# Hymba trunk, eight cores: mixing products on half the array's columns, weight casts two events behind their load, the last tile's output by quarters

## The reference: what is computed

```python
proj = h @ w_in[l]                       # 2048 -> 5632 columns: q | k | v | gate_a | u | v_s | gate_b
# group A: attention over the last 128 positions, 16 query heads, 4 key heads, RMS norm per head,
#          ALiBi penalty, a learned sink per head; the result times silu(gate_a)
# group B: u = gelu(z_u), v = gelu(z_v), 16 heads of 64 channels, chunks of 128 positions
mixed = einsum('hts,bnshc->bnthc', tril(w_s), v) + b_s      # one 128x128 matrix per head
sgu = u * mixed * silu(gate_b)
x = x + concat([attn, sgu]) @ w_out[l]
```

## Time and profile before

| | us |
|---|---|
| unprofiled runs | 7987.17, 8267.01, 8987.27 |
| median of these | 8267.01 |
| the profiled execution, its own time | 7963.68 |
| its span on the slowest core (core 5), first to last instruction | 7962.0 |
| spans of the eight cores | 7927.1 to 7962.0 |
| PE busy | 7752.7 (97%) |
| ACT busy | 3153.9 (40%) |
| DVE busy | 2864.1 (36%) |
| POOL busy | 645.4 (8%) |

### The profile page before, as it was taken

One profiled execution on the slowest core, in us unless ns is written; L12 is line 12 of the kernel. 1 busy time (PEld: TensorE's weight loads), 2 busy tenths in 40 slices (PEclk: granted clock), 3 DMA queues, 4 the chain that ended last, 5 costly groups with the idle time before them and its releaser, 6 DMA issues.

```text
span 7962.0 us, 140270 instructions; the slowest of 8 cores (7927.1 to 7962.0 us)
## 1 busy us (share of the span) xinstructions
PE 7752.7 (97%) x51494; PEld 4698.3 (59%) x51494; DVE 2864.1 (36%) x4126; ACT 3153.9 (40%) x5272; POOL 645.4 (8%) x622
## 2 busy tenths in 40 slices
PE   5899999999999999999999999999999999999999
PEld 3456555556666655666566665556666666665555
DVE  2523333433333334323333333344323433233333
ACT  1334444433333344434443344444433443233332
POOL 0000000000000000000000000000000000000000
PEclk8999999999999999999999999999999999999999
DMA  9988877786776777887876678777886665555554
GB/s 271 305 279 266 263 252 248 253 253 239 244 249 233 249 250 251 267 282 257 256 256 228 239 255 266 245 251 247 273 257 222 222 229 198 205 188 201 185 181 159
DMA packets 394284, 1925.05 MB, mean 242 GB/s; under 512 B 33680, under 2 KB 37904, under 8 KB 202768
## 3 DMA queue, kind: packets, MB, share of 16 engines
q1 hardware_dynamic: 346640, 1815.92, 69.1%
q10 hardware_dynamic: 46976, 100.17, 3.5%
HBM read 1650.68 MB, written 265.29 MB: 241 GB/s over the span
## 4 chain that ended last, share of the span: by engine, by line
PE 89%; DMA 5%; ACT 2%; SPq 1%; DVE 1%; issue 1%; ACTq 0%; DVEq 0%; POOL 0%
PE pp L283 87%; PE pp L286 2%; SPq L289 1%; DMA m_wslot<-scr 1%; DMA m_cst<-w_in 1%; DMA m_cst<-w_out 1%; ACT m_hb L274 1%; DVE m_qs L274 1%; DVE m_hb L274 0%; DMA m_xs<-x 0%; ACT m_sqf L274 0%; ACT m_cb L274 0%; ACTq L289 0%; DMA m_xr<-w_in 0%; DMA m_wslot<-w_out 0%
## 5 line engine op out<-in xcount | busy, mean ns | idle before, releaser
L283 PE MATMUL pp<-m_hT,m_wslot 128*128 128x512 bf16 (+1 forms) x13824 | 2849.1, 365 | 55.8 <-ACT m_ex L274 17.5
L283 PE MATMUL pp<-m_wslot,m_hT 128*128 128x256 bf16 x21344 | 2373.3, 273 | 37.8 <-DVE m_wslot L274 24.2
L283 PEld LDWEIGHTS pp<-m_wslot,m_hT 128*128 128x128 bf16 x21344 | 2089.6, 98 | 292.0 <-issue 40.3
L283 PEld LDWEIGHTS pp<-m_hT,m_wslot 128*128 128x128 bf16 x13824 | 1351.1, 98 | 1422.5 <-issue 115.2
L274 DVE TENSOR_TENSOR m_tf<-pp,m_bias 64x512 f32<-64x512 f32 (+1 forms) x576 | 373.0, 648 | 2303.7 <-PE pp L283 2239.1
L274 DVE TENSOR_TENSOR m_xr<-m_xr,pp 128x512 f32<-128x512 f32 x1064 | 705.2, 680 | 1009.9 <-PE pp L283 1008.2
L283 PE MATMUL pp<-m_wslot,m_zu 128*128 128x512 bf16 x4256 | 968.1, 381 | 19.8 <-DVE m_xr L274 19.6
L283 PE MATMUL pp<-m_wslot,m_ga 128*128 128x512 bf16 x4256 | 955.2, 381 | 8.6 <-DMA m_wslot<-scr 4.6
L283 PEld LDWEIGHTS pp<-m_wslot,m_zu 128*128 128x128 bf16 x4256 | 395.4, 98 | 574.1 <-issue 137.6
L283 PEld LDWEIGHTS pp<-m_wslot,m_ga 128*128 128x128 bf16 x4256 | 409.6, 98 | 491.9 <-issue 42.9
L274 POOL TENSOR_TENSOR m_zu<-m_tf,m_gbs 128x512 bf16<-128x512 f32 (+1 forms) x288 | 312.0, 1083 | 3737.0 <-DVE m_tf L274 3359.9
(11 more groups left out here) (49 smaller groups left out, 3451.5 us busy)
## 6 DMA issues: line engine op xcount, KB each, us to landing
m_wslot<-scr SPq DMA_DIRECT2D x1054, 1024.0 KB, 8.9
m_cst<-w_in SPq DMA_DIRECT2D x147, 1024.0 KB, 15.4
x_scr<-m_xr SPq DMA_DIRECT2D x100, 1024.0 KB, 17.6
m_xs<-x_scr SPq DMA_DIRECT2D x100, 1024.0 KB, 6.6
m_xr<-x_scr SPq DMA_DIRECT2D x99, 1024.0 KB, 10.0
scr<-m_cb ACTq DMA_DIRECT2D x180, 512.0 KB, 9.8
m_xr<-x SPq DMA_DIRECT2D x33, 1024.0 KB, 17.3
out<-m_xr SPq DMA_DIRECT2D x33, 1024.0 KB, 10.3
```

The source lines that it names most:

```text
L283: S.op("pe", lambda e: e.matmul(out, lhsT=lhsT, rhs=rhs, start=start, stop=stop), reads=reads, writes=writes)
```

## The change

Three edits. (1) In the gate_b stage both projections of a group come first, and then the mixing of both head pairs. For each block and head there is one matmul with 64 stationary columns and 128 moving columns, writing 64 partitions of one PSUM bank; the two heads of a pair use the two halves of the array's columns. The bias is then added in one DVE instruction of 128 partitions. (2) A conversion event casts the unit loaded two events before, and then loads into the buffer that this cast has read. At a layer end one unit is cast if two are loaded. (3) The last tile's output is stored by quarters of a block as soon as each is added.

```diff
@@ -425,13 +425,10 @@
 
 
 
-        conv = {"list": [(l, u) for l in range(1, DEPTH) for u in UNITS], "k": 0, "e": 0, "n": 0, "steps": 1, "loaded": None, "on": False}
+        conv = {"list": [(l, u) for l in range(1, DEPTH) for u in UNITS], "k": 0, "e": 0, "n": 0, "steps": 1, "loaded": [], "on": False}
 
         def conv_cast():
-            if conv["loaded"] is None:
-                return
-            l, unit, k = conv["loaded"]
-            conv["loaded"] = None
+            l, unit, k = conv["loaded"].pop(0)
             kind, g, q = unit
             src, Bsrc = cst[k][:, :], Bcst[k]
             if kind == "in":
@@ -456,13 +453,15 @@
             if conv["e"] * (len(conv["list"]) + DEPTH) < conv["n"] * conv["steps"]:
                 return
             conv["n"] += 1
-            conv_cast()
-            if conv["k"] < len(conv["list"]):
+            more = conv["k"] < len(conv["list"])
+            if len(conv["loaded"]) > (1 if more else 0):
+                conv_cast()
+            if more:
                 l, unit = conv["list"][conv["k"]]
                 k = conv["k"] % 2
                 conv["k"] += 1
                 load_unit("c%d" % k, l, unit, cst[k][:, :], Bcst[k])
-                conv["loaded"] = (l, unit, k)
+                conv["loaded"].append((l, unit, k))
 
         def next_w():
             i = wst["used"]
@@ -754,23 +753,25 @@
                 s = next_w()
                 if g < nb and not (l == 0 and ti == 0):
                     load_xr(g)
+                us = []
+                for cc in range(2):
+                    b = proj_B(s, cc, nb)
+                    u = turn("g")
+                    us.append(u)
+                    ACT([PB[b]], [Bgbs[u]], out=gbs[u][:, 0:cols], in_=bank(b)[:, 0:cols], func=AF.Silu)
                 for cc in range(2):
                     j = 2 * g + cc
-                    b = proj_B(s, cc, nb)
-                    u = turn("g")
-                    ACT([PB[b]], [Bgbs[u]], out=gbs[u][:, 0:cols], in_=bank(b)[:, 0:cols], func=AF.Silu)
-                    bp = nextpair()
-                    pv = pp[bp // 2][:, :].rearrange("p (n f) -> p n f", n=4)
+                    b = nextbank()
                     for n in range(nb):
-                        MM([Bz[2 * n + j // 4], BwsT], [PB[bp + n // 2]], pv[:, n, :], zv[:, n, j * 128:(j + 1) * 128],
-                           wsT[:, 2 * j:2 * j + 2, :], True, True)
+                        for half in range(2):
+                            c0 = j * 128 + 64 * half
+                            MM([Bz[2 * n + j // 4], BwsT], [PB[b]], bank(b)[64 * half:64 * half + 64, n * 128:n * 128 + 128],
+                               zv[:, n, c0:c0 + 64], wsT[:, 2 * j + half, :], True, True)
+                    u = us[cc]
                     u2 = turn("t")
-                    for half in range(2):
-                        rows = slice(64 * half, 64 * half + 64)
-                        TT("dve", [PB[bp], PB[bp + 1], Bbias], [Btf[u2]],
-                           out=tf[u2][rows, 0:cols].rearrange("p (n t) -> p n t", n=nb),
-                           in0=pv[rows, 0:nb, half * 128:half * 128 + 128],
-                           in1=bias[rows, j, :].unsqueeze(1).to_broadcast([64, nb, 128]), op=ADD)
+                    TT("dve", [PB[b], Bbias], [Btf[u2]], out=tf[u2][:, 0:cols].rearrange("p (n t) -> p n t", n=nb),
+                       in0=bank(b)[:, 0:cols].rearrange("p (n t) -> p n t", n=nb),
+                       in1=bias[:, j, :].unsqueeze(1).to_broadcast([128, nb, 128]), op=ADD)
                     TT("dve", [Btf[u2], Bzu[j]], [Btf[u2]], out=tf[u2][:, 0:cols], in0=tf[u2][:, 0:cols], in1=zu[:, j, 0:cols], op=MUL)
                     TT("pool", [Btf[u2], Bgbs[u]], [Bzu[j]], out=zu[:, j, 0:cols], in0=tf[u2][:, 0:cols], in1=gbs[u][:, 0:cols], op=MUL)
 
@@ -833,6 +834,9 @@
                             MM([Bws[s], bsrc(e, n)], [PB[b]], bank(b), src[:, e, n * 128:(n + 1) * 128], w[:, e, :], e == 0, e == 7)
                         xo = xr[n][:, 512 * q:512 * q + 512]
                         TT("dve", [PB[b], Bxr[n]], [Bxr[n]], out=xo, in0=xo, in1=bank(b), op=ADD)
+                        if base == G_OA and last["final"]:
+                            blk = b0 + n - NH
+                            DMA("xq%d_%d" % (n, q), [Bxr[n]], [], out=A["out"][blk * 128:blk * 128 + 128, 512 * q:512 * q + 512], in_=xo)
                         yield
 
             if l == 0 and ti == 0:
@@ -862,7 +866,8 @@
             rest = None
             if last["layer_end"] and l + 1 < DEPTH:
                 conv["on"] = False
-                conv_cast()
+                if len(conv["loaded"]) > 1:
+                    conv_cast()
                 layer_bias(l + 1, "sp")
                 k = conv["k"] % 2
                 DMA("c%d" % k, [], [Bcst[k]], out=cst[k][:, :].rearrange("p (h s) -> p h s", h=16), in_=A["w_s"][l + 1].rearrange("h t s -> t h s"))
@@ -901,7 +906,8 @@
                 blk = b0 + n
                 dst = A["x_scr"][blk] if l + 1 < DEPTH else A["out"][(blk - NH) * 128:(blk - NH) * 128 + 128, :]
                 DMA("xo%d" % n, [Bxr[n]], [Bx[blk]], out=dst, in_=xr[n][:, :])
-            stores.extend(lambda n=n: flush(n) for n in range(nb))
+            if not last["final"]:
+                stores.extend(lambda n=n: flush(n) for n in range(nb))
 
         every = [(l, ti, b0, nb) for l in range(DEPTH) for ti, (b0, nb) in enumerate(layer_tiles(l, DEPTH, NOWN))]
         conv["steps"] = sum((NG - 4 if k + 1 == len(every) or every[k + 1][0] == l else NG - 8)
@@ -910,7 +916,7 @@
             nxt = every[k + 1] if k + 1 < len(every) else None
             end = nxt is None or nxt[0] != l
             nprep = 0 if nxt is None else nxt[3] + (1 if end and l + 1 < NH else 0)
-            tile(l, ti, b0, nb, {"nprep": nprep, "layer_end": end}, every[k - 1][3] if ti > 0 else 0)
+            tile(l, ti, b0, nb, {"nprep": nprep, "layer_end": end, "final": nxt is None}, every[k - 1][3] if ti > 0 else 0)
         for f in stores:
             f()
         S.emit()
```

## The result

Over twelve runs the changed kernel has a median of 7965.9 us and the kernel before, over as many, 8299.2. Executions in which the four cores of a die, or all eight, ran at a lower granted clock are in these medians, but such cores are left out of all that follows. What is left of the changed kernel lies at 7948 to 7972, and its ratio to the kernel before is **0.9968, 95% interval 0.9954 to 0.9982**: a gain of 0.32%, about 25 us, where the sum said 35 us (0.44%).

The account below looks back on a forecast made before the run. PE, with 89% of the chain of waits, was taken to bound the kernel. The sum was 7963.7 - 25 - 27 + 21 - 4 = 7929 us, own range 7895 to 7975, all cases 7890 to 8000, upper end taken at 8270.

Parts of the forecast that it names:

- The base: Start of the sum: all terms set against the profiled execution of 7963.7 us, not the runs' median 303 us above it.
- the layer ends: Next layer's w_s load waits for a cast on ACT, so PE stands: 5 us plus about 16, 21 more in all.
- Part 1: Mixing in gate_b: 117 us removed, 60 added for half-array pairs and 32 for 288 mode changes, so 25 us less.
- Rival (a): Mixing pairs bound by issue or unhidden loads, 0.112 us each: 59 us worse, 7988 us; chance 0.14.
- Part 2, the gain: Casts no longer wait for loads on ACT: 19.7 us of PE waits and 7.5 of half clock go, 27 less.
- half clock: PE ran at half clock after four of its waits behind late casts; 7.5 us expected back.
- ACT's waits should all but vanish: Casts on ACT: a load has about five groups, 34 us, less its start; the longest landing was 29.0.
- so it hides this, and I put it at nothing: SP's loads behind its wait for ACT's cast: weight loads wanted three groups (21 us) later, so no cost.
- rival (b): Casts' gain lost to late weight loads on SP; PE's `wslot` waits grow by 10 us: 7966 us; chance 0.12.
- Rival (c): Layer ends not paid, as ACT reaches the cast early or w_s lands sooner: 7908 us; chance 0.08.
- Part 3: Last addition to span end, 6.9 us before: about 3 with one 256 KB store left, so 4 us less (1 to 6).
- the bound of 0.028 us an instruction: PE issue limit read from transposes: a mixing pair's four instructions would take 0.112 us, 119 in all; taken as upper bound.

Follow-up runs that it names:

- e1: Kernel before with only the gate_b mixing on half the columns: ratio 0.9959, mean span 27 us below the kernel before.
- e4: Changed kernel with each head pair's mixing right behind its own projection, 576 mode changes instead of 288: mean span 1 us below the kernel before.
- e3: Kernel before with only the last tile's output stored by quarters: ratio 1.0004, mean span 3 us below the kernel before.
- e2: Kernel before with only the casts two events behind their load: mean span 7942.2 us, 11 below the kernel before.
- e5: Changed kernel with the layer end's cast put before the os stage of the layer's last tile: ratio 0.9945, mean span 44 us below the kernel before.
- e7: Changed kernel with the layer end's cast before the os stage and loads issued a group later: ratio 0.9972, mean span 38 us below the kernel before.
- a2: Changed kernel as it is, run again on another chip: mean span 7912.5 us, 29 below the kernel before.
- e6: Changed kernel with each conversion load issued one group after its event's cast: ratio 0.9968, mean span 24 us below the kernel before.
- e8: Changed kernel with conversion loads of a quarter of the bytes, single execution: mean span 7889.5 us, 56 below the kernel before.

## Why the prediction was right or wrong

**The base: wrong, and this is the step that failed.** The number on record, 7929, rests on one execution of 7963.7 us. The four runs of the kernel before that the ratio takes lie at 7977 to 7987, so I had started 13 to 23 us low, and all eight of the changed kernel (7948 to 7972) lie above 7929. Set beside the median of 8267 that was shown, 7929 reads as 4% less, while the sum only ever said 0.44% and the runs showed 0.32%. What failed is the step "all terms below are set against the profiled execution", without carrying the result over to the runs by a ratio. As a ratio the forecast is 0.9956, which lies inside the measured interval (0.9968, 0.9954 to 0.9982). Of the terms, three were mis-sized: the wait for weights put at nothing (5 us measured), the layer ends (21 put, 11 measured) and the end (4 put, 2.2 measured); they are taken up below.

**Part 1: right, term by term.** Forecast were 25 us; 24 come from the tiles of layer 3 (25 x 0.80 + 11 x 0.36), 27 from e1. A pair costs 0.056 us, as read, and a change 0.11 (e4). Rival (a), 59 us worse, is out. What the prediction passed over is in the earlier trace rows: 8.8 us of waiting for `tf` ahead of the mixing products, which went in the first tile and mostly came back there as waits for weights (e1).

The Trainium skill has a rule in its page "TensorEngine Tiling (Array Packing)", section "Key Properties": a change of mode drains the engine. e4 shows what a change costs, 0.11 us; that it is a drain no run shows. By the same page of the Trainium skill, section "Restrictions", column tiling turns off the fast weight load. Here no cost of that is seen: eight pairs and two changes in 0.67 us leave no room over 0.056 a pair.

**Part 2, the gain: right.** I had 19.7 us of waits and 7.5 of half clock, from core 5. On the mean core 18.3 of waits went, and what is left of the stretches' lengths after waits and mixing is 7.4 (0.7 + 2.7 + 3.1 + 0.9), which fits the half clock. The granted clock bears this out: length times what the clock lacks of full speed, summed over the four stretches, is 15.9 us before and 14 to 15 in e1 and e3, but 6.3 after and 4 to 6 in e2, e5, e7 and a2. This takes in time in which PE stands, so it is an upper reading. The waits for `ex` were to be near 8 us on core 5 and are 9.4. "ACT's waits should all but vanish" holds for the loads alone; 33 us of waiting for the store from `cb` stand, at no cost to PE that a run shows.

**Part 2, "so it hides this, and I put it at nothing": right for SP, a little wrong for PE.** SP's wait for ACT is hidden (e6), so rival (b)'s mechanism is refuted. PE's wait for `wslot` was to be near 27 us and over 40 for rival (b). On core 5 it is 29.0, but on the mean core it rose from 24.9 to 41.3, 8.7 of it in the first tile. Of the rest about 5 us go with the new casts, a term that the sum had at 0, and they come from the conversion loads' transfers (e8), not from SP. So the rival's sign was there and its cause was not.

**Layer ends: right in mechanism, too large.** Forecast were waits for w_s of 12.6 and 13.6 us; on core 5 they were 10.9 and 12.6, since the load took 9.0 and 9.8 us and not 10.8. In all 21 was forecast. Against the kernels that cast as before it is 11: 10 in tile 17 and 1 in tiles 7 and 8, where the weight wait was absorbed as said. Half of the misfit is that tile 17 was 5 us shorter in the one profile that I had read than in e1 and e3. Mending them gave 15 (e5), a part of it beyond what the kernel before had. Rival (c) is out.

**Part 3: too large.** It gave 2.2 us (6.9 to 4.7 on all cores) and not 4. After the last addition, with only 256 KB to go, 4.7 us pass to the end of the span, where I had taken 3. Bytes are not what sets this: on core 0 the DMA engines move 58 GB/s in these 4.7 us, and the earlier trace rows's stretch of 12 us before had 350. What does set it is open.

**The sum.** With the measured terms: -24 - 25.7 + 5 + 11 - 2.2 = -36 us, the same as the forecast's -35. That is luck: the price of the layer ends, put 10 us too high, is made up by the waits for weights, put 5 too low, and by the gains of the three parts, put 1, 1 and 2 too high. The executions gave 29 less on the mean span (a2, error 3.9), 27 + 11 + 3 = 41 as the sum of the parts alone (error 5), 18 in the profile after, and the slowest core 25 less, with an interval from 14 to 37. These don't contradict each other, but nor do they fix the whole to better than some 10 us. Part of the scatter is the start-up, which no term of mine covers: the first tile took 403.8 us before, 408.4 after and 393 to 408 in the other profiles. What sets it is not settled.

## What to carry to other kernels

What a cast reads should have landed long before the cast comes up in the queue of an engine with other work; but a load moved behind that cast inherits its place in the queue, and wherever something else wants the buffer (here the next layer's w_s) that price is paid in full: look for all users of a double buffer before making it two deep. Half-array products side by side cost what one whole product of as many columns costs, plus 0.11 us for each change of mode: group them until the changes are few. And where cores differ by 30 us from run to run, forecast the ratio, not the time, and read the mean over the cores.

## What the runs showed that I had not expected

- A pair of half-array matmuls with 128 columns and a load each runs at the distance of one whole-array matmul, although it issues four instructions in 0.056 us; the bound of 0.028 us an instruction that I had read from the transposes is none.
- A change of mode costs 0.11 us next to 128-column and next to 512-column products alike (0.90 us for eight, e4).
- 1 MB weight loads with a median of 9.0 us to landing took 25 to 28 us four times in a row (core 2 of the changed kernel, from 1605 us on). The three groups of distance, 21 us, don't cover that.
- With the loads landed in time, the casts wait for the store of the cast before: 33 us on ACT's mean core, 11 before. There is one buffer `cb`.
- With a last store of 256 KB, 4.71 us pass from the last addition to the end of the span, the same within 0.01 us on all eight cores (4.36 in e3, which has the kernel before's mixing and casts; why it is less is open).
